# Hybrid encoder trunk: the recurrence's projections in three rounded passes, its turns a step later, beta and decay beside the grouped keys, and a tenth expert slot

## What is computed

```
for l in range(2):
    h = rmsnorm(x, attn_norm_w[l])
    g_qkv, g_z, g_b, g_a, d_q, d_k, d_v, c_q, c_k, c_v, gate_raw = split(h @ w_in[l])
    y_a = gated_deltanet(silu(short_conv5(g_qkv)), beta=sigmoid(g_b), decay from g_a)   # 4 heads of 128
    y_b = differential_attention(d_q, d_k, d_v)                     # 4 heads, two softmax maps each
    y_c = grouped_attention(c_q, c_k, c_v)                          # 8 query heads, 2 key heads
    x = x + (sum of sigmoid(gate_i) * (y_i @ P_i)) @ w_out[l]
    x = x + sum over the token's 2 experts of weight * (silu(h2 @ w1[e]) * (h2 @ w3[e])) @ w2[e]
return rmsnorm(x, final_norm_w)
```

## Time and profile before

| | us |
|---|---|
| median of 3 runs (lowest, highest) | 1653.12 (1648.83, 1657.19) |
| the profiled execution, its own time | 1650.25 |
| its span, first to last instruction | 1648.4 |
| PE busy / DVE / ACT / POOL | 1322.1 / 669.1 / 465.6 / 117.8 |
| mean granted TensorE clock | 0.938 |

### The profile page before, as it was taken

How to read it: one execution, slowest core, us unless ns; L and a number is a source line. 1 busy time by engine, 2 the same in 40 slices (tenths; PEclk the granted TensorE clock), 3 DMA queues, 4 the chain that set the end, 5 groups by cost and what they waited for, 6 DMA issues and landing times. The chain is left out here.

```text
span 1648.4 us, 46417 instructions
## 1 busy us (share of the span) xinstructions
PE 1322.1 (80%) x19424; PEld 1018.9 (62%) x19425; DVE 669.1 (41%) x1620; ACT 465.6 (28%) x948; POOL 117.8 (7%) x106
## 2 busy tenths in 40 slices
PE   6998899988866676667889989998889776666765
PEld 5786777775644454445567777877666554444543
DVE  6657757654211111111276668565622211111112
ACT  3445546432100000000045455444501100000001
POOL 2002430000000000000010025200000000000000
PEclk9998899999989999998999989999999999999998
DMA  9531016487999999999974210354889999999996
GB/s 302 207 143 52 1 36 221 162 348 267 427 429 427 429 428 428 429 429 428 420 267 173 102 52 2 119 188 170 350 327 429 429 428 428 429 428 428 428 428 278
DMA packets 76724, 490.22 MB, mean 297 GB/s; under 512 B 12879, under 2 KB 15463, under 8 KB 52071
## 3 DMA queue, kind: packets, MB, share of 16 engines
q1 hardware_dynamic: 76646, 489.16, 73.0%
HBM read 488.09 MB, written 1.05 MB: 297 GB/s over the span
## 5 line engine op out<-in xcount | busy, mean ns | idle before, releaser
L1907 PE MATMUL ps<-ring,arena 128*32 128x128 f32 x5760 | 209.0, 308 | 153.8 <-DMA ring<-in_expert_w_up_dram 95.0
L1907 PEld LDWEIGHTS ps<-ring,arena 128*32 128x32 f32 x5760 | 182.0, 124 | 175.5 <-DMA ring<-in_expert_w_up_dram 104.1
L2070 DVE COPY arena<-ps 128x256 f32<-128x256 f32 x68 | 28.9, 425 | 329.8 <-PE ps L1880 329.7
L1982 ACT ACTIVATE arena<-ps 128x128 f32<-128x128 f32 x66 | 18.3, 277 | 484.6 <-PE ps L1907 484.6
L1907 PE MATMUL ps<-arena 128*32 128x128 f32 x2688 | 92.1, 296 | 67.6 <-DMA arena<-in_expert_w_up_dram 42.4
L1907 PEld LDWEIGHTS ps<-arena 128*32 128x32 f32 x2688 | 79.6, 119 | 77.8 <-DMA arena<-in_expert_w_up_dram 46.4
L460 POOL TENSOR_TENSOR small<-small,cst 128x8 f32<-128x8 f32 (+1 forms) x21 | 27.7, 1320 | 1253.3 <-DVE small L705 462.3
L1696 DVE TENSOR_TENSOR w_low<-ring,w_high 128x512 fp32r<-128x512 f32 x128 | 86.8, 705 | 50.2 <-ACT w_high L1627 50.2
L1627 ACT ACTIVATE w_high<-ring 128x512 fp32r<-128x512 f32 x128 | 78.7, 634 | 85.7 <-PE ps L1564 68.8
L1925 PE MATMUL ps<-ring,arena 128*32 128x256 f32 x1440 | 87.6, 382 | 5.2 <-DMA ring<-in_expert_w_down_dram 3.1
L1880 PE MATMUL ps<-xn,arena 128*32 128x256 f32 x1088 | 85.0, 435 | 5.9 <-DVE arena L2065 5.7
(11 more groups left out here) (351 smaller groups left out, 2448.0 us busy)
## 6 DMA issues: line engine op xcount, KB each, us to landing
ring<-in_expert_w_gate_dram SPq DMA_DIRECT2D x44, 2048.0 KB, 41.8
ring<-in_expert_w_up_dram SPq DMA_DIRECT2D x44, 2048.0 KB, 40.6
ring<-in_expert_w_down_dram SPq DMA_DIRECT2D x44, 2048.0 KB, 40.6
ring<-in_w_in_dram SPq DMA_DIRECT2D x28, 2048.0 KB, 8.5
arena<-in_expert_w_gate_dram SPq DMA_DIRECT2D x20, 2048.0 KB, 41.8
arena<-in_expert_w_up_dram SPq DMA_DIRECT2D x20, 2048.0 KB, 40.9
arena<-in_expert_w_down_dram SPq DMA_DIRECT2D x20, 2048.0 KB, 40.7
ring<-in_w_out_dram SPq DMA_DIRECT2D x4, 2048.0 KB, 7.8
```

Of the source, the lines that this page charges most:

```text
L1907: ins = pe.matmul(bank_b[32 * g:32 * g + 32, u * P:(u + 1) * P], xg[:, c], w[:, u, c, g], start=(c == 0), stop=(c == KC - 1))
L2070: v.tensor_copy(rows, bank_a[:, 0:256]).then_inc(m_rows, 1)
```

## The change

- The recurrence's projections (`proj`) go in three rounded passes like all others. Per head (12 in a layer, numbered i) ACT writes `g_w_high` (1024 elements per partition, `gdn_high`) into one of four buffers, POOL writes the remainder into the ring slot in place (`gdn_low`), and PE does 24 fp32r products of 256 columns instead of 8 plain ones. Heads 0 and 1 are split at the end of the projection block, 2 to 11 in the attention block.
- The low part of h is made once, at the start of the projection, in place of h; the four POOL passes at the end of attention go.
- The turns of the recurrence's groups come a step later in `pieces`, the second half of the v projection a step earlier, and DVE's `l2norm(0)` moves from step 2 to step 3.
- Beta and decay ride as 16 more columns of the CKV chunks (272), their 16 plain products go; the CKV chunks' low parts are POOL's work, no longer DVE's.
- Experts: a tenth slot lies over x and hT, which are free from the router on. It takes the gate weights of expert 3 before `h_nb`; the ring slot of gate weights that it spares is then one expert ahead. On PE the first two rounds of the expert loop are written out apart from it.

```
+        for q, (u, c, cols) in enumerate(chunks_b):                       # project_pool
+            if u == U_CKV:
+                pool.wait_ge(b_hi, q + 1)
+                pool.tensor_tensor(w_lo[u % UNITS][:, c * 512:c * 512 + cols], unit8(u)[:, c, 0:cols], b_w_hi[:, q % 4, 0:cols].bitcast(F32),
+                                   ALU.subtract).then_inc(b_kv_lo, 1)
         roots(pool, b_asked, b_root, [hrs[:, 0:8], hrs[:, 0:8], hrs[:, 0:2], hrs[:, 0:2]])
+        for i in range(2):
+            gdn_low(pool, i)
...
+    def gdn_high(act, l, i):
+        if i % HEADS == 0:
+            unit_landed(act, l, U_GQ + i // HEADS)
+        act.activation(g_hi[i % 4], gdn_columns(i), ACT.Copy).then_inc(d_hi, 1)
+
+    def gdn_low(pool, i):
+        pool.wait_ge(d_hi, i + 1)
+        pool.tensor_tensor(gdn_columns(i, low=True), gdn_columns(i), g_hi[i % 4].bitcast(F32), ALU.subtract).then_inc(d_lo, 1)
...
-        pieces = [[("proj", 0, 0), ("proj", 0, 1)], [("proj", 1, 0), ("proj", 1, 1)], [("proj", 2, 0), ("tok", 0, 0), ("tok", 0, 1)],
-                  [("tok", 1, 0), ("tok", 1, 1)], [("proj", 2, 1)], [], [("back", 0, 0), ("back", 0, 1)],
+        pieces = [[("proj", 0, 0), ("proj", 0, 1)], [("proj", 1, 0), ("proj", 1, 1)], [("proj", 2, 0)],
+                  [("tok", 0, 0), ("tok", 0, 1), ("proj", 2, 1)], [("tok", 1, 0), ("tok", 1, 1)], [], [("back", 0, 0), ("back", 0, 1)],
...
                         for h in (2 * w, 2 * w + 1):                      # PE, fill("proj", g, w)
+                            i = HEADS * g + h
+                            pe.wait_ge(d_lo, i + 1)
...
+                                pe.matmul(out, w_high[:, c], HT_hi[:, c], start=(c == 0), stop=False)
+                                pe.matmul(out, w_low[:, c], HT_hi[:, c], start=False, stop=False)
+                                ins = pe.matmul(out, w_high[:, c], HT_lo[:, c], start=False, stop=(c == KC - 1))
...
                     for piece in pieces[s]:                               # ACT
                         empty(*piece)
+                        if piece[0] == "proj":
+                            pair = 2 * piece[1] + piece[2] + 2
+                            for i in range(2 * pair, min(2 * pair + 2, 3 * HEADS)):
+                                gdn_high(act, l, i)
...
+                sp.wait_ge(h_xn, NT)                                      # SP, before the router's count
+                sp.wait_ge(h_kept, 1)
+                load_expert(sp, l, SETS, 3 * SETS)
                 sp.wait_ge(h_nb, 1)
...
-                jobs(pe, job)
+                jobs(pe, job, apart=2)
```

More of the change, by code:

```diff
@@ L136, in encoder_trunk @@
     hT = sb("hT", KC * SEQ)
+    assert start_of["hT"] == start_of["x_sb"] + 4 * NT * D_MODEL
+    tenth = nc.alloc_sbuf_tensor_at("tenth_slot", [P, 4096], F32, offset=start_of["x_sb"])
     xn = sb("xn", NT * D_MODEL)
@@ L340, in encoder_trunk @@
     m_gate = sem("m_gate_done")
-    m_land = [sem(f"expert_landed{n}") for n in range(3 * SETS)]
+    m_land = [sem(f"expert_landed{n}") for n in range(3 * SETS + 1)]
     def cleared(pool, *stages):
@@ L399, in load_more @@
             (kn_w, gqa_k_norm_w[one].broadcast_to([P, 64])),
-            (wba, w_in[one, :, C_BA:C_BA + 16].rearrange("o (c p) n -> p (o c) n", c=KC)),
         ):
@@ L423, in load_expert @@
             w = (expert_w_gate, expert_w_up)[n % 3].rearrange("l e (p c) f -> (l e) p c f", c=KC)
-            dst = expert_slot(n).rearrange("p (o c f) -> p o c f", o=1, c=KC)
+            dst = (tenth[:, :] if n == 3 * SETS else expert_slot(n)).rearrange("p (o c f) -> p o c f", o=1, c=KC)
         else:
@@ L475, in encoder_trunk @@
     roped = 8
-    chunks_b = [(u, j, 256 if u == U_CKV else 512) for u in streamed_b for j in range(KC)]
+    chunks_b = [(u, j, KV_BA if u == U_CKV else 512) for u in streamed_b for j in range(KC)]
     used_at.update({u: (b_used, KC * (n + 1)) for n, u in enumerate(streamed_b)})
@@ L537, in project_tensor @@
                 pe.wait_ge(*((b_hl, c // 2 + 1) if c < 4 else (b_hlp, c // 2 - 1)))
-            pe.wait_ge(b_lo, q + 1)
+            if u == U_CKV:
+                pe.wait_ge(b_kv_lo, c + 1)
+            else:
+                pe.wait_ge(b_lo, q + 1 if n == 0 else q + 1 - KC)
             w, w_low = b_w_hi[:, q % 4, 0:cols], w_lo[u % UNITS][:, c * 512:c * 512 + cols]
@@ L543, in project_tensor @@
                 pe.matmul(bank, HT_hi[:, c, tok], w_low, start=False, stop=False)
-                ins = pe.matmul(bank, b_HT_lo[:, c, tok], w, start=False, stop=(c == KC - 1))
+                ins = pe.matmul(bank, HT_lo[:, c, tok], w, start=False, stop=(c == KC - 1))
             ins.then_inc(b_used, 1)
-            if q == KC - 1:
-                pe.wait_ge(p_early, 16 * 3 * (l + 1))
-                for t in range(NT):
-                    for cc in range(KC):
-                        ins = pe.matmul(ps[6][:, t * 16:(t + 1) * 16], HT[:, cc, t * P:(t + 1) * P], wba[:, cc],
-                                        start=(cc == 0), stop=(cc == KC - 1))
-                ins.then_inc(b_ba, 1)
             if c == KC - 1 and n >= 1:
@@ L726, in project_vector @@
             n = q // KC
-            if q >= 4:
+            if q >= 4 and u != U_CKV:
                 w_low(q)
@@ L789, in filled @@
             return fills_at[kind, g, 1] + 1
[L791 removed]
+        f_hi, f_lo, f_used = (sem("f_" + n) for n in ("w_high", "w_low", "w_used"))
         f_sq_b, f_sq, f_yn, f_on, f_zc, f_zs, f_ya, f_t, f_yh, f_yl, f_sig, f_m, f_chain = (
@@ L898, in _ @@
             def _(act):
+                for i in (2, 3):
+                    gdn_high(act, l, i)
                 act.activation(beta.rearrange("p d t h -> p t d h"), bar[:, :, 0:8].rearrange("p t (d h) -> p t d h", d=2),
@@ L1046, in weigh @@
                     ins.then_inc(c_prob, 1)
-                work = {0: [(convolve, 0, 0), (convolve, 0, 1)], 1: [(convolve, 1, 0), (convolve, 1, 1)], 2: [(l2norm, 0)],
-                        3: [(convolve, 2, 0)], 4: [(convolve, 2, 1)], 5: [(l2norm, 1)]}
+                work = {0: [(convolve, 0, 0), (convolve, 0, 1)], 1: [(convolve, 1, 0), (convolve, 1, 1)],
+                        3: [(l2norm, 0), (convolve, 2, 0)], 4: [(convolve, 2, 1)], 5: [(l2norm, 1)]}
                 weigh(0)
@@ L1730, in gate_up, with jobs @@
             return pair.rearrange("p (u c g f) -> p u c g f", u=2, c=KC, g=4)
-        def jobs(eng, body):
+        def jobs(eng, body, apart=0):
             J = eng.alloc_register(f"jobs{l}")
@@ L1743, in of_expert @@
                     eng.reg_add(J, J, 1)
-            with eng.Fori(0, N_EXPERTS // SETS) as i:
+            for i in range(apart):
+                for k in range(SETS):
+                    of_expert(i, k)
+            with eng.Fori(apart, N_EXPERTS // SETS) as i:
                 for k in range(SETS):
@@ L1769, in count, with refill @@
                     sp.reg_add(ended, ended, n)
-                def refill(i, k, load):
+                def refill(i, k, load, gate=True):
                     count(i, k)
-                    sp.wait_ge(m_gate, sp.snap(ended))
-                    load(i, 3 * k)
+                    if gate:
+                        sp.wait_ge(m_gate, sp.snap(ended))
+                        load(i, 3 * k)
                     sp.wait_ge(m_gu, sp.snap(ended))
@@ L1792, in _, with next_but_one @@
                     sp.dma_start(fw, final_norm_w.rearrange("(o d) -> o d", o=1).broadcast_to([P, D_MODEL])).then_inc(z_w, 16)
-                with sp.Fori(0, N_EXPERTS // SETS - 1) as i:
+                def next_but_one(i, n):
+                    load_expert(sp, l, (i + 2) * SETS if n == 0 else (i + 1) * SETS + n // 3, n)
+                for k in range(SETS):
+                    refill(0, k, next_but_one)
+                for k in range(SETS):
+                    refill(1, k, next_expert, gate=k > 0)
+                with sp.Fori(2, N_EXPERTS // SETS - 1) as i:
                     for k in range(SETS):
```

58 lines of the change are left out of this document (35 added, 23 removed).

## The result

The changed kernel takes 1679.53 us (1674.10 to 1680.43, 4 runs) against 1654.17 for the kernel before; ratio 1.0159, 95% interval 1.0141 to 1.0177. It is 25 us slower; 1674 was forecast. Its profiled execution has a span of 1678.6 us, 30.2 more than before.

The account below looks back on a forecast made before the run. It took the weight stream to bound the expert stage, and PE, then DVE's chain from 118 us, the attention stage. 1650.25 + 32 (attention) + 0 (projection) - 8.8 (tenth slot) = 1673.5, given as 1674 us; range 1651 to 1690, bounds 1635 to 1708.

Parts of the forecast that it names:

- PE's passes: Recurrence's projections on PE: products 0.12 us apart, 5.7 us for two heads, 34 per layer in place of 42.8.
- POOL's pass: Attention block: a two-input POOL pass of 1024 elements takes 2.36 us, ten passes 23.6 us.
- the CKV pass: Projection stage: each of eight POOL passes for the CKV low parts takes about 0.75 us, 6 in all.
- The turns with DVE: Attention: DVE instructions with two SBUF inputs wait out POOL's passes in turn; first convolution ends at 123.2, +11.8 us.
- The walk with the new order: Attention followed engine by engine: half convolution ends at 160.8 in place of 145.05, stage about 14.5 us later per layer.
- by the order alone, +4 us: Attention without POOL holding DVE: conv 0 at 108, conv 1 at 125, and the order adds 4 us.
- not held: Rival: L1015 shares with POOL without waiting, attention costs only order and a little clock; 1651 us, chance 0.17.
- Clock: Attention: PE idles longer, so proj(2, 1) and later steps run partly at 1.2 GHz; +1.5 us, bounds 0 and +8.
- Projection stage, 0: Projection stage: work taken off PE and DVE is offset by a later first rope root; 0, bounds -3 and +3 per layer.
- Tenth slot, -8.8: Expert stage: one more load in idle DMA time ends the stream 4.9 us earlier, +0.5 against, per layer; -8.8 in all.
- the small loads of the next layer queue behind the tenth: Expert stage: one of the costs set against the tenth slot's gain, together taken at +0.5 us per layer.
- the likeliest case: The forecast's own case, 1674 us with DVE and POOL taking turns: chance 0.60, range 1662 to 1688.

Follow-up runs that it names:

- experiment 6: The kernel before with only beta and decay beside the grouped keys and the CKV chunks' low parts on POOL: 1649.05 us against 1652.13, ratio 0.9985.
- experiment 2: The changed kernel with POOL's passes over the recurrence's weights reading one SBUF input, writing weight times 2^-12: 1658.74 us, ratio 1.0037.
- experiments 5 and 8: 5: the changed kernel with the old order and the recurrence's low parts on DVE, 1637.54 us; 8: the kernel before with only the tenth slot, 1647.57 us.
- experiment 3: The kernel before with only the new order, projections still plain products: 1675.66 us, ratio 1.0137.

## Why the prediction came out as it did

Time (1674 against 1679.5), direction, and the stage of the loss were right. The profiled execution became 30.2 us longer where the sum had 32 + 0 - 8.8 = 23.2: attention +31.8, the two last blocks -3.9 in place of -8.8, the projections +1.5, recurrence and gates +0.8 for which nothing was set. So the term that was mis-sized is the tenth slot; and inside the attention term, right in total, the division between POOL and the order was wrong. The parts of the attention stage add up from the runs like this, in us per layer:

| | attention, layers 1 and 2 |
|---|---|
| plain products, old order (the kernel before; with the tenth slot alone; experiment 6) | 91.6, 88.2; 89.9, 89.9; 89.8, 89.9 |
| the same, new order | 102.6, 102.6 |
| three passes, low parts on DVE, old order | 86.5, 86.6 |
| three passes, low parts on POOL, old order | 92.5, 92.5 |
| three passes, low parts on POOL, new order (the change; without its tenth slot) | 105.0, 106.5; 106.5, 104.8 |
| three passes, one input on POOL, new order | 98.8, 98.4 |

Order +12.8, three passes with DVE's low parts -3.3, POOL in place of DVE +6.0: 89.8 + 12.8 - 3.3 + 6.0 = 105.3, against 105.0 and 106.5 measured. The order costs about the same with plain products (12.8) and in the changed kernel (12.5 and 14.0), which fits that each sits at its own place on DVE's chain: the turns before 122, the order's gap behind 138. The new order with the low parts on DVE was not run.

- *PE's passes* (34 us per layer in place of 42.8, 0.12 us apart): right at full clock; in the first layer of the trace they take 36.9, 1.9 of the difference in proj(2, 1) at half clock. *POOL's pass* of 2.36 us measured 2.48, the CKV pass of 0.75 measured 0.78. The working was luckier than that: the row of 1892 ns, read as a pass with one streamed input, is L1703, which multiplies a tensor by itself, and the real one-input pass of experiment 2 takes 2.8 us, more than the two-input one. The product shown for the CKV pass should read 0.53 x 1080, which gives 0.77; as it stands it gives 1.3.
- *The turns with DVE*: right in kind (experiment 2) and in size at the first convolution (+10.4, forecast +11.8). POOL's seven passes ended at 117.4 (forecast 117.3), in part by luck: they were expected without a break and with an instruction of DVE between two, and had no such instructions between them but two waits for ACT (1.23 and 0.57 us). DVE got ten of its 20 instructions done by then and not five. At the end of the second group +3.5 was left, forecast +5.0; against low parts made by DVE it is 6.0 at the end of the stage. The rule quoted from the Trainium skill (SBUF — State Buffer, "Who interferes with whom") holds where POOL's pass has two inputs: the longest tap took 2.63 us in place of 0.48. It also counts any GpSimd instruction that reads SBUF, and there experiment 2 disagrees on the length of the wait: the pass read SBUF, and a held tap took 1.14 us, not a whole pass of 2.8. The measurement decides.
- *The walk with the new order* was right to 1.5 us at every point compared here. *The step that took it apart was wrong*: "by the order alone, +4 us" without the turns. The walk itself has 5.0 from the turns and 10.8 from the order (15.8 at the half convolution). The +4 can only be the order net of the relief by the faster products (its second convolution ends at 125, 5.5 us before 130.5, and 1.3 come off between 15.8 and 14.5), and was named wrongly. The runs have 12.8 for the order and 3.3 for the relief, so 9.5, and experiment 2, with short holds in place of the turns, has 98.6 - 89.8 = 8.8. So the rival "not held", at 1651, was priced too low (experiment 2 took 1658.7), and the text put the loss on POOL ("decides the change"), where of the 18.8 us that the two add two thirds are the order's.
- *Clock*: taken at +1.5 per layer, mostly for proj(2, 1). From 140.48 to the turn at 148.06 it took 7.6 us in place of 5.7, +1.9. Right.
- *Projection stage, 0*: alone it is -2.5 us in all (experiment 6), in the trace of the changed kernel +1.5. Bounds held.
- *Tenth slot, -8.8*: over-sized, and the step that failed is that a stream that ends 4.9 us earlier ends the block as much earlier in both layers. In the second layer -4.2 (forecast -4.4); in the first nothing in the changed kernel (+0.4). The named risk, "the small loads of the next layer queue behind the tenth", was priced at part of 0.5 us; they stand at one of the places where the gain goes, and the end of the stream, where the last weights take 3.1 us longer to land, is another. How the 4.4 us divide stays open. The rows that pointed to the first place were there: SP's ten issues of L418 end at 389.48 and the first refill follows at 390.78, with 1.3 us to spare, and all of them moved behind another load.
- *Range and chances*: 1651 to 1690 held it; the likeliest case's own range did too. The lower bound of the sum is 1642 (1650.25 + 8 - 6 - 9.8), not 1635.

## What to carry to other kernels

When a stage is a chain that hops between engines written in fixed order, price a move by the next wait of every engine that the moved piece now stands in front of, and price each edit alone and together from the same walk: a right total can hide wrong parts, and then the wrong part gets undone. Before work is put on an idle POOL, look at what DVE runs at that time: beside a POOL pass with two SBUF inputs the taps and the L1046 that read SBUF were held for a pass, the maxima that read PSUM were not. If DVE has gaps of its own, the same pass may be cheaper there (1.22 us against 2.48 here, and nothing held). A gain in the stream of loads is not yet a gain in time: follow it to the last load's landing. A load that is put into an idle time of the DMA engines also moves everything that its issuing engine does next.

## What the runs showed of the hardware

- While POOL passes with two SBUF inputs follow each other, DVE gets one instruction that reads SBUF done per pass (eight taps 11.97 us in place of 3.63; two L1046, with one SBUF tensor as input, 4.99 in place of 0.60); two L1017, which read PSUM, take 1.29 us there and without POOL alike. With one input on POOL's side a tap takes at most 1.14 us in place of 0.48, once per pass, though the POOL pass of the same 1024 elements is then longer, 2.8 us against 2.5.
- Issuing a DMA is not a fixed cost: the same small load (`attn_norm_w`) took 0.30 us on SP before and, right behind the tenth load of 2 MB, 0.44 with the old order, 0.60 to 0.67 in experiments 5 and 8 and 1.95 in the changed kernel; the router's weights took 1.20 us on SP and 9.51 on ACT while SP's large loads were under way.
- After 8.3 and 9.4 us of idle time PE began its dense products at half clock: 0.21 us apart in the changed kernel (granted clock 0.50), and 8.95 us for 32 in experiment 3 (granted 0.55 in the first 4 us, then 1.00), where 64 took 14.08 at full clock.
